# New values of a gated delta rule from k times the old state: W and its scaled keys taken out of a decoder layer

## The reference, cut to what matters

```python
rhs = jnp.concatenate([vc * bc[..., None], kb * jnp.exp(gc)[..., None]], axis=-1)
sol = lax.linalg.triangular_solve(a_mat, rhs, left_side=True, lower=True, unit_diagonal=True)
u_c = sol[..., :dv]
w_c = sol[..., dv:]
...
def step(state, inp):
    v_new = u_i - jnp.einsum('bhcd,bhde->bhce', w_i, state)
    o = jnp.einsum('bhcd,bhde->bhce', q_i, state) + jnp.einsum('bhij,bhje->bhie', a_i, v_new)
    state = state * jnp.exp(gl)[..., None, None] + jnp.einsum('bhcd,bhce->bhde', k_e, v_new)
    return state, o
```

## Time and profile before

| | |
|---|---|
| median of 3 runs | 2343.08 us (2342.4 to 2344.78) |
| the profiled execution | 2344.14 us, of which the span is 2342.5 us |
| TensorE busy in the span | 2278.0 us, 97% |
| VectorE, ScalarE, GpSimd busy | 759.7, 371.7 and 587.2 us |
| mixers stage, roughly | from 360 to 710 us in the span |
| a tail, from the start of `PU` to `gates_columns` | 13.5 us, four times |

### The profile page before, as it was taken

One profiled execution on the slowest core, in us unless ns is written; L12 is line 12 of the kernel. 1 busy time (PEld: TensorE's weight loads), 2 busy tenths in 40 slices (PEclk: granted clock), 3 DMA queues, 4 the chain that ended last, 5 costly groups with the idle time before them and its releaser, 6 DMA issues.

```text
span 2342.5 us, 36437 instructions
## 1 busy us (share of the span) xinstructions
PE 2278.0 (97%) x14408; PEld 1920.2 (82%) x14409; DVE 759.7 (32%) x1747; ACT 371.7 (16%) x837; POOL 587.2 (25%) x808
## 2 busy tenths in 40 slices
PE   8999998999996999999999999999999999999997
PEld 5664447779765999999999999998887887878876
DVE  2234776545632153222222222221221221222224
ACT  2222643223220010001111111110000000000002
POOL 1132222322423122222222222232222222222222
PEclk9999998999997999999999999999999999999999
DMA  7000103011017766777787888899999999999996
GB/s 259 1 1 18 36 18 132 19 46 46 28 47 263 239 214 199 240 238 242 250 257 250 280 288 280 287 282 322 329 323 334 332 323 330 331 324 336 324 328 230
DMA packets 375013, 505.00 MB, mean 216 GB/s; under 512 B 12744, under 2 KB 288652, under 8 KB 374793
## 3 DMA queue, kind: packets, MB, share of 16 engines
q1 hardware_dynamic: 359976, 458.50, 58.6%
q0 software_dynamic: 14864, 44.14, 7.2%
HBM read 471.12 MB, written 34.13 MB: 216 GB/s over the span
## 4 chain that ended last, share of the span: by engine, by line
PE 68%; DMA 0%; DVE 0%; issue 0%; POOL 0%; POOLq 0%; DVEq 0%
PE ps L1685 44%; PE ps L1712 12%; PE ps L1697 10%; PE ps L1664 2%; PE ps L1673 1%; DMA arena<-h_dram,arena 0%; DVE arena L1937 0%; POOL out L1564 0%; DVE arena L1943 0%; DVE arena L1923 0%; DVE arena L1830 0%; POOL small L225 0%; DVE small L222 0%; DVEq L1940 0%; POOLq L1564 0%
## 5 line engine op out<-in xcount | busy, mean ns | idle before, releaser
L1685 PEld LDWEIGHTS ps<-arena 128*128 128x128 f32 x8192 | 1031.1, 191 | 9.3 <-issue 7.7
L1685 PE MATMUL ps<-arena 128*128 128x128 f32 (+15 forms) x8192 | 1037.6, 288 | 0.8 <-DVE arena L1830 0.8
L1854 DVE TENSOR_SCALAR arena<-ps,arena 128x128 f32<-128x128 f32 (+15 forms) x256 | 94.7, 370 | 1112.4 <-PE ps L1685 1111.6
L1524 POOL TENSOR_TENSOR arena<-arena 128x128 f32<-128x128 f32 (+15 forms) x256 | 131.6, 514 | 879.1 <-DVEq L1861 879.1
L1596 ACT ACTIVATE arena<-arena 128x128 f32<-128x128 f32 (+15 forms) x256 | 83.3, 325 | 1214.5 <-DVE arena L1854 1214.5
L1712 PE MATMUL ps<-arena 128*128 128x224 f32 (+14 forms) x1920 | 272.4, 303 | 0.0
L1712 PEld LDWEIGHTS ps<-arena 128*128 128x128 f32 x1920 | 270.1, 189 | 0.2
L1697 PE MATMUL ps<-arena 128*128 128x512 f32 x544 | 236.3, 592 | 0.0
L1697 PEld LDWEIGHTS ps<-arena 128*128 128x128 f32 x544 | 102.0, 190 | 122.0 <-issue 121.7
L503 PE MATMUL ps<-arena 128*128 128x384 f32 (+1 forms) x512 | 171.5, 494 | 2.1 <-DVE arena L605 2.1
L503 PEld LDWEIGHTS ps<-arena 128*128 128x128 f32 x512 | 97.4, 193 | 68.1 <-issue 2.4
(11 more groups left out here) (262 smaller groups left out, 1592.8 us busy)
## 6 DMA issues: line engine op xcount, KB each, us to landing
arena<-in_exp_w_gu SPq DMA_DIRECT2D x256, 1024.0 KB, 7.7
arena<-in_exp_w_down SPq DMA_DIRECT2D x64, 2048.0 KB, 8.9
arena<-in_exp_b_down SPq DMA_DIRECT2D x17, 512.0 KB, 10.6
arena<-in_x SPq DMA_DIRECT2D x16, 512.0 KB, 9.1
arena<-in_w_in SPq DMA_DIRECT2D x8, 1024.0 KB, 7.1
h_dram<-arena SPq DMA_DIRECT2D x16, 512.0 KB, 2.7
arena<-in_w_out SPq DMA_DIRECT2D x1, 4096.0 KB, 12.9
arena<-h_dram SPq DMA_DIRECT2D x8, 512.0 KB, 7.2
```

Source lines behind the costliest of these rows:

```text
L1524: v.tensor_tensor(gmn[m % 2][:, 0:n], gmn[m % 2][:, 0:n], umn[m % 2][:, 0:n], ALU.mult).then_inc(S("gum", m % 2), 1)
L1685: last = t_.matmul(bank(m % 4)[:, q * CAP:q * CAP + n], wslot[g][:, k, 256 * q + c:256 * q + c + P], xT[:, k, 0:n], start=(k == 0), stop=( ...
L1854: v.tensor_scalar(gmn[r][:, 0:n], bank(m % 4)[:, 0:n], of[:, m:m + 1], LIMIT, ALU.add, ALU.min).then_inc(S("gmn", r), 1)
```

## The change

`kbg`, `wT` and `nW` go. TensorE multiplies k itself (`qkvT[:, 4 + h, ...]`, which lies ready in the layout wanted) with `Sm` into bank 4s + 3 (semaphore `kS`). VectorE's new `fresh_rows(s)` takes that times beta gamma of each row, less beta v, in four instructions with 128 columns each (semaphore `rhs`), in place of `vb[s]`. One group of products with `Um[s]` then gives minus the new values, and ScalarE's copy to `EV[s]` takes factor -1. The order of the tail on TensorE becomes old state, values, new state for s = 0, and then the same for s = 1.

```diff
@@ ScalarE, finish(i)
-                for s in range(2):
-                    act.wait_ge(S("kt", s), i + 1)
-                    for h in range(H):
-                        last = a.activation(kbg[s][:, h * P:(h + 1) * P], bank(4 * s)[:, h * P:(h + 1) * P], ACT.Copy,
-                                            scale=bx_all[:, 2 * i + s, h:h + 1])
-                    last.then_inc(S("kbg", s), 1)
...
-                for s in range(2):
-                    act.wait_ge(S("wT", s), i + 1)
-                    a.activation(nW[s], bank(4 * s + 3), ACT.Copy, scale=-1.0).then_inc(S("nwT", s), 1)
                 for s in range(2):
                     act.wait_ge(S("vnew", s), i + 1)
-                    a.activation(EV[s], bank(4 * s), ACT.Copy).then_inc(S("vn_sb", s), 1)
+                    a.activation(EV[s], bank(4 * s), ACT.Copy, scale=-1.0).then_inc(S("vn_sb", s), 1)
@@ TensorE, chunk(i); start(i, s) waits for rhs in place of nwT, and level 2 no longer for kbg
-                for s in range(2):
-                    pe.wait_ge(S("Ul", s), i + 1)
-                    four(bank(4 * s + 3), kbg[s], Um[s], S("wT", s))
-
-                def values(s):
-                    for h in range(H):
-                        c_ = slice(h * P, (h + 1) * P)
-                        t_.matmul(bank(4 * s)[:, c_], Um[s][:, c_], vb[s][:, c_], start=(h == 0), stop=False)
-
                 def old_state(s):
-                    pe.wait_ge(S("nwT", s), i + 1)
+                    pe.wait_ge(S("Tl", s), 6 * i + LEVELS - 1)
+                    if s == 0 and i:
+                        pe.wait_ge(S("state"), 2 * i)
                     if s == 1:
                         pe.wait_ge(S("state"), 2 * i + 1)
                     for h in range(H):
                         c_ = slice(h * P, (h + 1) * P)
-                        last = t_.matmul(bank(4 * s)[:, c_], nW[s][:, c_], Sm[:, c_], start=False, stop=(h == H - 1))
-                    last.then_inc(S("vnew", s), 1)
+                        last = t_.matmul(bank(4 * s + 3)[:, c_], qkvT[:, 4 + h, cols(2 * i + s)], Sm[:, c_], start=True, stop=True)
+                    last.then_inc(S("kS", s), 1)
...
+                def values(s):
+                    pe.wait_ge(S("Ul", s), i + 1)
+                    pe.wait_ge(S("rhs", s), i + 1)
+                    four(bank(4 * s), Um[s], vb[s], S("vnew", s))
+
...
+                old_state(0)
                 values(0)
-                values(1)
-                old_state(0)
                 new_state(0)
                 old_state(1)
+                values(1)
                 new_state(1)
@@ VectorE, chunk(i)
-                            dve.wait_ge(S("kbg", s), i + 1)
+                            dve.wait_ge(S("kt", s), i + 1)
...
+                def fresh_rows(s):
+                    dve.wait_ge(S("kS", s), i + 1)
+                    dve.wait_ge(S("vb", s), i + 1)
+                    for h in range(H):
+                        c_ = slice(h * P, (h + 1) * P)
+                        last = v.scalar_tensor_tensor(vb[s][:, c_], bank(4 * s + 3)[:, c_], bx_all[:, 2 * i + s, h:h + 1],
+                                                      vb[s][:, c_], ALU.mult, ALU.subtract)
+                    last.then_inc(S("rhs", s), 1)
...
+                fresh_rows(0)
                 states(0)
+                fresh_rows(1)
                 normed(0)
                 states(1)
```

More of the change, by code:

```diff
@@ L988, in start @@
                     pe.wait_ge(S("vn_sb", s), i)
-                    pe.wait_ge(S("nwT", s), i)
+                    pe.wait_ge(S("rhs", s), i)
                 for h in range(H):
@@ L1056, in chunk @@
                         if l == 2:
-                            pe.wait_ge(S("kbg", s), i + 1)
                             pe.wait_ge(S("ke", s), i + 1)
```

## The result

Over 20 runs of each kernel taken in turn, the changed kernel takes 2347.16 us (2344.12 to 2351.95) and the kernel before 2343.27 us (2339.51 to 2345.48): a ratio of 1.0020, 95% interval 1.0013 to 1.0026. The ratio and its interval come from the runs of both kernels together; the two medians by themselves differ by 3.9 us, 0.17%. By the medians the change stays under the 0.2% that was set as the bound of "no change that can be told"; the interval leaves out 1 and reaches past that bound, so the changed kernel is a little slower, and on which side of 0.2% it lies stays open. The profiled execution took 2349.64 us, of which the span is 2348.0.

The account below looks back on a forecast made before the run. TensorE, busy 2278.0 of 2342.5 us, was taken as the bound, with each pair's tail read as a chain. Four pairs at 1.08 us gave +4.3 us on 2343.08, so 2347.4 us, range 2343.5 to 2352.0.

Parts of the forecast that it names:

- The order and its chain: New order laid over the last pair's tail, start to start, with the old trace's latencies: a pair 1.08 us longer.
- forecast of the pauses: TensorE's tail: about 0.6 us ahead of each `values`, about 0.7 to 0.9 us ahead of each product with `ke`.
- 0.95 and 3.8 us of waits: TensorE's pauses in one tail, claimed to grow from 0.95 us before the change to 3.8 us after it.
- The price of `fresh_rows`: Four VectorE instructions in the tail's path, priced like line 1271: 1.12 us, TensorE starting 1.27 us after their start.
- TensorE's two groups: Two `wT` groups a pair leave TensorE, 1.79 us of its work, yet the pair was forecast longer.
- `kbg` at nothing: ScalarE's eight `kbg` copies a pair, taken as hidden by VectorE's own work: their removal counted as no gain.
- `QD` times the state: TensorE's tail: needs the logits copied, `lg_sb` there at 652.44 us, ahead of 653.97 where wanted.
- `normed(0)`: VectorE: held up by `fresh_rows(1)` to 662.0 us, but what follows is wanted only after `gates_columns`, 1.08 us later too.
- Hidden pauses (faster): Tail: other products fill the waits, so four tails lose two groups each, 7.2 us, 2335.9 us; chance 0.10, whole or part.
- The clock in the tail (slower): TensorE's clock falls once in each tail, 6.5 us more, 2353.9 us; chance 0.22.
- The total: Whole kernel: +4.3 us to 2347.4 us, +0.18%; faster 0.08, same 0.48, slower 0.44.

Follow-up runs that it names:

- one-head kernel: Changed kernel with `fresh_rows` working for one head of four, so three heads' values are wrong; 2776.0 us, not comparable, tail 13.34 us.
- filler: Changed kernel with one more, unread group of products with U behind each values group; 2347.57 us, 1.0024 of the kernel before.
- order-only: Kernel before, W kept, with `values(1)` moved behind `new_state(0)`; 2337.74 us, 0.9984 of the kernel before.
- mixed: Chunk 0 of each pair as in the change, chunk 1 as in the kernel before with W; 2335.62 us, 0.9974 of the kernel before.
- changed kernel with signals by head: Changed kernel, but `fresh_rows` signals each head and TensorE's product with U waits head by head; 2340.57 us, 0.9991 of the kernel before.
- mixed form with signals by head and the logits apart: Chunk 0 new, chunk 1 with W; `fresh_rows(0)` and state signalled per head, chunk 0's logits moved ahead of level 5's last products; 2334.08 us.

## Why the prediction was right

**The order and its chain.** The step that mattered, laying the new order over the last pair with the latencies of the earlier trace rows, gave 1.08 us a pair; measured were 1.15. Step by step the offsets from `PU`'s start were: `fresh_rows(0)` 2.88 predicted, 2.94 measured; `values(0)` 4.15 and 4.21; product with `ke` 6.00 and 6.03; k times the state for chunk 1 8.43 and 8.49; `values(1)` 10.86 and 10.93; `gates_columns` 14.57 and 14.64. The error is 0.06 in the two `PU` groups, which take 1.85 us and not 1.79 up to the next group, and hundredths elsewhere that cancel. Only the forecast of the pauses was off in size: about 0.6 us was said to stand ahead of `values`, and the rows show 0.42, beside 0.69 ahead of the product with `ke`. The prediction found its 0.95 and 3.8 us of waits by taking 0.895 us for each group off the tail; the profile's brackets have 0.41 and 2.63 us. The sum does not hang on it, since it goes from start to start.

**The price of `fresh_rows`.** Line 1271 was the right row to take: 1.13 us for four against 1.12, and 1.27 us to TensorE's start in both. The advice of the Trainium skill in "VectorE: DVE Perf Modes", section on the TRN2 errata, on tiles of 512 columns or more points at the right place. Its figure for PSUM reads gives, as an estimate, 0.26 us for one instruction of 128 columns and 1.03 us for four; that was low here, and the row decides. The one-head kernel shows where the difference lies: one such instruction alone takes 0.35 us and four take 1.13, so each further one adds 0.26 us, which agrees with the page, while the first costs 0.35. What neither said is that splitting need not cost as much: with a signal for each head the four small instructions overlapped with the product, and the tail became 1.31 us shorter.

**TensorE's two groups.** They were counted at nothing, since the longer chain would cover them, and the filler shows it: 14.64 us with two groups more in a pair, and 14.64 without.

**`kbg`, `QD`, `normed`.** `kbg` at nothing: shown. `QD` times the state did not wait for `lg_sb`: in the last pair it starts 0.89 us after k times the state (656.25 to 657.14), with no pause. `normed(0)` came later and delayed nothing: the last pair's projection starts 1.98 us after `gates_columns` in both kernels (664.77 to 666.75 us, and 669.04 to 671.02), and the first pair's 2.69 us after it in both (417.02 to 419.71, and 416.19 to 418.88).

**The rivals.** Hidden pauses (faster) did not come. The clock in the tail (slower) did not come: it was granted in full, 1.00, with TensorE busy for 12.02 of 14.64 us. The Trainium skill, "TensorE: Matmul & The Clock Gate", section on a second failure mode, tells of a clock that goes back and forth when TensorE pauses briefly between groups; in the tail that was not seen, with pauses of 0.4 to 0.7 us.

**The total.** Predicted 2347.4 us, measured 2347.16; the median rose by 3.9 us, where 4.3 was worked out and the tails have 4.6. That the times agree to 0.2 us is luck: a fall of the clock makes a pair 1.6 us longer, and the runs of both kernels lie 6 to 8 us apart. Luck too is on which side of the bound the result came: the prediction itself put 4.3 against 4.7 us, with nearly even chances. The mechanism, a longer chain in each tail, is shown by the rows and by the experiments, and does not rest on that.

## What to carry to other kernels

Before work is taken off the busiest engine, find the chain that leads from one step's state to the next one's, and ask of each instruction of the new form whether it stands on it. In this kernel the work ahead of the state filled waits (two groups more a pair cost nothing in the changed tail); the algebra with fewer products put one of them, and a step on another engine, behind the state, and was dearer. The best form used each where it was cheap. Where small instructions hand over to another engine, signal each of them: here it turned a tail 1.15 us longer than before into one 0.16 us shorter, with no less work.

## What the runs showed that I had not expected

- A change of values ahead of a routing step can change the amount of work: the one-head kernel took 433 us more than the kernel before, though its part up to the experts is no longer (their products begin at 731.60 us, and at 731.56 before).
- The medians of the order-only and mixed kernels fell by 2.3 and 2.6 us more than their tails did, and that of the changed kernel with signals by head by 1.5. Among the last three pairs their profiles have one fall, none and none. Whether a shorter pair makes falls rarer, or the runs had luck, stays open.
- The shortest of all, the mixed form with signals by head and the logits apart, is 2334.08 us, 0.9965 (0.9952 to 0.9979) of the kernel before, with four tails 6.2 us shorter in sum.
